# Block 1's attention with transposes ahead of scores, and copies ahead of row factors

## The reference, cut to what matters

```python
s_c = einsum(qb, k_c) * scale                      # 31 compressed blocks of keys
p_c = masked_softmax(s_c, c_end[None, :] <= tpos[:, None])
o_c = einsum(p_c, v_c)
...                                                # selected blocks: s_s, p_s, o_s
s_w = einsum(qb, kw) * scale                       # window of 512 keys
p_w = masked_softmax(s_w, m_w)
o_w = einsum(p_w, vw)
return gb[..., 0:1] * o_c + gb[..., 1:2] * o_s + gb[..., 2:3] * o_w
```

## Time and profile before

| | before |
|---|---|
| median of three runs | 2811.77 us |
| profiled execution, its own time | 2809.11 us |
| its span | 2807.3 us |
| TensorE busy (share of the span) | 2681.9 us (96%) |
| TensorE weight load | 2198.0 us (78%) |
| VectorE | 1571.4 us (56%) |
| ScalarE | 1055.5 us (38%) |
| GpSimd | 1178.2 us (42%) |
| attention of block 1 | 278 to 517 us of the span |

### The profile page before, as it was taken

How to read it: one execution, slowest core, us unless ns; L and a number is a source line. 1 busy time by engine, 2 the same in 40 slices (tenths; PEclk the granted TensorE clock), 3 DMA queues, 4 the chain that set the end, 5 groups by cost and what they waited for, 6 DMA issues and landing times.

```text
span 2807.3 us, 38071 instructions
## 1 busy us (share of the span) xinstructions
PE 2681.9 (96%) x13128; PEld 2198.0 (78%) x13128; DVE 1571.4 (56%) x2448; ACT 1055.5 (38%) x1826; POOL 1178.2 (42%) x592
## 2 busy tenths in 40 slices
PE   7999888899999999999999999999899999999998
PEld 6877666778888878878887788888687778888886
DVE  7996666564343376466665745545623447653364
ACT  4224777633222254443334411112525553211133
POOL 3432585244444444355423344444442214444443
PEclk9999999999999999999999999999999999999999
DMA  3242000133222232221102322222231112322222
GB/s 133 99 141 83 16 24 9 53 120 106 92 96 97 97 113 102 82 99 61 61 31 91 136 92 96 97 97 91 95 110 53 46 46 97 122 96 97 98 97 90
DMA packets 67460, 242.88 MB, mean 87 GB/s; under 512 B 7772, under 2 KB 10117, under 8 KB 66573
## 3 DMA queue, kind: packets, MB, share of 16 engines
q1 hardware_dynamic: 59760, 215.37, 22.6%
q10 hardware_dynamic: 7580, 25.91, 2.6%
HBM read 232.80 MB, written 6.35 MB: 85 GB/s over the span
## 4 chain that ended last, share of the span: by engine, by line
issue 47%; PE 34%; POOL 14%; DVE 2%; ACT 2%; POOLq 0%; DMA 0%; DVEq 0%; SPq 0%; ACTq 0%
POOL w_lo L442 12%; PE bank L2585 9%; PE bank L2587 9%; PE bank L2586 9%; PE bank L3133 2%; PE bank L3122 2%; POOL stat L469 1%; PE bank L2907 1%; POOL stat L466 1%; PE bank L2800 1%; PE bank L2894 0%; PE bank L2771 0%; ACT tmp L974 0%; DVE big L1925 0%; POOLq L446 0%
## 5 line engine op out<-in xcount | busy, mean ns | idle before, releaser
L442 POOL TENSOR_TENSOR w_lo<-raw,w_hi 128x1024 fp32r<-128x1024 f32 x398 | 972.4, 2443 | 1561.2 <-ACT w_hi L589 1439.9
L2585 PE MATMUL bank<-act,w_hi 128*128 128x512 f32 x3128 | 1259.0, 403 | 51.9 <-POOL w_lo L442 14.6
L2587 PE MATMUL bank<-act,w_lo 128*128 128x512 f32 x3128 | 1227.0, 392 | 0.0
L2586 PE MATMUL bank<-act,w_hi 128*128 128x512 f32 x3128 | 1226.6, 392 | 0.0
L589 ACT CAST w_hi<-raw 128x1024 fp32r<-128x1024 f32 x396 | 415.5, 1049 | 900.7 <-PE bank L2587 888.9
L2585 PEld LDWEIGHTS bank<-act,w_hi 128*128 128x128 f32 x3128 | 592.5, 189 | 199.7 <-issue 31.6
L2587 PEld LDWEIGHTS bank<-act,w_lo 128*128 128x128 f32 x3128 | 592.2, 189 | 126.9
L2586 PEld LDWEIGHTS bank<-act,w_hi 128*128 128x128 f32 x3128 | 592.9, 190 | 121.0 <-issue 5.5
L1685 DVE TENSOR_TENSOR X<-X,bank 128x512 f32 x56 | 38.5, 688 | 241.3 <-PE bank L2587 241.3
L2076 DVE CAST act<-tmp 128x512 f32 x64 | 142.4, 2225 | 10.0 <-DVE tmp L2072 5.2
L1837 DVE SCALAR_TENSOR_TENSOR bank<-big,cols,bank 128x512 f32<-128x512 f32 x174 | 117.0, 748 | 0.4
(11 more groups left out here) (427 smaller groups left out, 2962.5 us busy)
## 6 DMA issues: line engine op xcount, KB each, us to landing
raw<-in_w_dram SPq DMA_DIRECT2D x402, 512.0 KB, 3.4
act_f<-head_rows ACTq DMA_DIRECT2D x8, 768.0 KB, 4.2
proj_rows<-big ACTq DMA_DIRECT2D x4, 1024.0 KB
big<-proj_rows ACTq DMA_DIRECT2D x2, 2048.0 KB, 9.2
X<-in_x_dram SPq DMA_DIRECT2D x4, 512.0 KB, 6.1
act_f<-in_cw1k_dram ACTq DMA_DIRECT2D x4, 512.0 KB, 4.2
cst<-in_consts_dram ACTq DMA_DIRECT2D x2, 648.5 KB, 7.9
X<-big ACTq DMA_DIRECT2D x8, 128.0 KB, 3.4
```

Source lines behind the costliest of these rows:

```text
L442: pool.tensor_tensor(w_lo[:, u], raw[:, u].rearrange("p (k n) -> p k n", k=KT), w_hi[:, u].bitcast(F32), ALU.subtract).then_inc(w_lo_ready, 1)
L2585: pe.matmul(o, l_hi, r_hi, start=start, stop=False)
L2586: pe.matmul(o, l_hi, r_lo, start=False, stop=False)
L2587: return pe.matmul(o, l_lo, r_hi, start=False, stop=stop)
```

## The change

Three loops are written in another order. No instruction is added or taken away, and no wait changes.

```diff
@@ ScalarE
                     if n < N:
                         scale_rows(n)
+                    if n + 1 < N:
+                        exps(n + 1)
...
                     if n % 8 in (2, 4) and n // 8 + 1 < NH // 2:
                         compressed_exp(n // 8 * 2 + 2 + (n % 8 == 4))
-                    if n + 1 < N:
-                        exps(n + 1)
@@ VectorE
                 maxima(0)
+                maxima(1)
...
                 for n in range(N + 3):
+                    later = n // 8 + 1 < NH // 2
+                    if 2 <= n < N + 2:
+                        keep_second_pt(n - 2)
                     if n < N:
                         row_factor(n)
-                    if 2 <= n < N + 2:
-                        keep_second_pt(n - 2)
-                    if n + 1 < N:
-                        maxima(n + 1)
...
+                    if later and n % 8 in (1, 3):
+                        compressed_shift(n // 8 * 2 + 2 + (n % 8 == 3))
+                    if n + 2 < N:
+                        maxima(n + 2)
+                    if later and n % 8 in (4, 6):
+                        compressed_sum(n // 8 * 2 + 2 + (n % 8 == 6))
@@ TensorE
                 scores(0)
+                scores(1)
                 for n in range(N + 2):
                     if n < 6 * KT:
                         gate_filler(n)
-                    if n + 1 < N:
-                        scores(n + 1)
+                    if 1 <= n <= N:
+                        transposes(n - 1)
+                    if n + 2 < N:
+                        scores(n + 2)
                     if n % 8 in (0, 2) and n // 8 + 1 < NH // 2:
                         compressed_scores(n // 8 * 2 + 2 + (n % 8 == 2))
                     if n % 2 and n >= 3:
                         values(n - 3)
-                    if 1 <= n <= N:
-                        transposes(n - 1)
```

## The result

| | before | changed |
|---|---|---|
| median of the runs | 2811.14 us | 2846.15 us |
| profiled execution, its own time | 2809.11 us | 2844.81 us |
| its span | 2807.3 us | 2843.0 us |
| attention, causal mask of the first scores (0.3 us behind their start) to end | 277.6 to 517.0 us | 275.6 to 553.3 us |

A forecast was written before the change was run, and what follows sets the result against it. Waits going round between engines, none full, were taken to bound the attention. Octet terms of 4, 6.5, 4 and 2 us, together 16.5, on the profiled 2809.1 gave 2826 us (52%), range 2793 to 2842.

The forecast's parts named there:

- the clock: Attention: as many falls of the granted clock as before, costed at nothing, with bounds of 6 us either way.
- the wait of the maxima: Attention, step 4 of an octet: VectorE's maxima (1.2 us) and compressed sum (1.25) stand ahead of the copy TensorE needs.
- The views and the loop: Attention: waits going round between engines bound it; the loop for one pair sums to 6.95 us before, 6.84 after.
- The 36.7 us ahead of the values: TensorE's idle ahead of the values in the attention, expected to fall near nothing, with 50 to 60 us ahead of transposes.
- The sum for the order, 16.5 us: Attention: slower by 4 us in octet 0, 1.3 in each of octets 1 to 5, 4 in octet 6, 2 in octet 7.
- The copy of an even tile now starts at the end of the values: Attention: this copy must wait for the previous pair's values, leaving only the gate product to hide it before the next transposes.
- ScalarE's edit at nothing: Attention: exponentials moved earlier give back 0.3 to 0.6 us at three steps, not waited for, so costed at nothing.
- Octets 6 and 7 at 4 and 2 us: End of the attention: octet 6, without gate products, 4 us longer; octet 7, without cast and compressed work, 2 us longer.
- Faster: Rival: 36.7 us ahead of the values go, 19 come back ahead of transposes, 18 us less, 2791; chance 22%.
- No change: Rival: both loops hold the same work and an order adds no buffer, so 2809, within 5; chance 18%.
- Much slower: Rival: waits between VectorE's maxima and copies pass 2.5 us in every octet, the clock falling each time, 2840; chance 8%.
- The long factor: VectorE's two-element factor multiplication: 0.44 us on average, long while GpSimd's taps run, in both orders, difference the same.

The follow-up runs named there:

- e5: Changed kernel with VectorE's maxima one tile ahead instead of two, TensorE's scores still two ahead: 2804.05 us, 0.9985 of the kernel before.
- e7: Changed kernel with values ahead of transposes again and maxima one tile ahead: 2801.66 us, 0.9976 of the kernel before.
- e4: Changed kernel with only the values put back ahead of the transposes, maxima still two ahead: 2855.96 us, 1.0172 of the kernel before.
- e11: Changed kernel run once more, unaltered, for a second profile: 2861.51 us, 1.0176 of the kernel before.
- e9: Changed kernel plus three idle matmuls of 512 columns at each of the attention's last 18 steps: 2838.39 us, 1.0097 of the kernel before.
- e1: Kernel before with ScalarE's edit alone, exponentials ahead of the compressed one and the gate's copy: 2808.7 us, 0.9999 of the kernel before.
- e13: Kernel before with VectorE's copy ahead of the factor and ScalarE's edit: 2791.45 us, 0.9933 of the kernel before.
- e10: Kernel before plus three idle matmuls of 512 columns at each of the attention's last 18 steps: 2812.8 us, 1.0011 of the kernel before.
- e2: Kernel before with VectorE's copy ahead of the row factor alone, maxima and scores one ahead: 2793.08 us, 0.9947 of the kernel before.
- e6: Changed kernel with VectorE's factor ahead of the copy again, maxima still two ahead: 2862.81 us, 1.0187 of the kernel before.
- e12: Changed kernel with the factor's multiplication as two instructions of one tensor input each: 2838.23 us, 1.0102 of the kernel before.

## Why the prediction was wrong

Two steps failed: the clock, which was put at no change, and the wait of the maxima, which was counted in one step of eight and stands in nearly all.

**The views and the loop.** That the stage is bound by waits that go round was right. The 36.7 us ahead of the values went (0.8 left), and came back ahead of the transposes: 50.5, where 50 to 60 was predicted. Reciprocal, ScalarE's copies (38.7 us for values) and octets of 30 us or more came as written. Octet 6 "near 28" did not: 37.6.

**The sum for the order, 16.5 us.** The octets at full clock in both profiles give +1.0 (octet 3). Against the mean of before's octets at full clock with gate products, 29.15, the three at 31.9, 30.0 and 31.9 are 2.1 longer; predicted was 1.3. Taking 0.43 per us at half clock out, the attention is 277.7 - 24.7 = 253.0 against 239.4 - 5.5 = 233.9: about 19 us for the order (17 to 21 if half clock costs 0.48 or 0.38 instead). The size was nearly right, and the reason given for it mostly wrong. "The copy of an even tile now starts at the end of the values" is in the trace (L1941 waits 29.6 us for values), but with maxima one ahead the same place of the values costs nothing that can be told from none (e5, e7), and moving them back alone repairs nothing (e4: by the same reckoning its order costs some 36 us, with 40 at half clock). What costs is that maxima wait in front of the next copy for scores that TensorE issues behind the transposes. I had this wait at step 4 alone, where the compressed sum stands with it; it is there 57 times in 64.

**The step that put the number out of its range is the clock: "I expect as many falls as before", bounds 6 us either way.** Half clock went from 12.8 to 57.4 us, worth 0.43 x 44.6 = 19 us, and to 91.0 in the second profile, 34 us. The shares of order and clock add up, by the way they are taken, to the 38.3 us by which the attention is longer; it also starts 2.0 us earlier. The argument was "two idles of about 2 us in an octet" and so no change. The two are there: 16 idles of 1.8 us or more ahead of the transposes in eight octets, up to 4.0, and three ahead of scores. But the kernel before had only 8 so long in its whole attention, one in most octets, and e5 has 5. Their number alone doesn't decide: e11 has 19 as well, with 91.0 us at half clock instead of 57.4, and e4 has 18 with only 40. The runs don't show which property of the waits decides it. They show where: octets 6 and 7 in both profiles, with no gate product among the waits, and that matmuls put there bring the clock back (e9).

**ScalarE's edit at nothing** was right (e1, e13). **Octets 6 and 7 at 4 and 2 us** measured 11.2 and 15.2, most of it clock: in e9, with 3 x 0.24 us more in each step, they are at 31.3 and 38.2, 2.3 and 0.2 above e10.

**The rivals.** *Faster*, 2791, is what VectorE's copy first gives by itself, on TensorE's old order (2793, e2), but the same list moved the maxima, and that decided. *No change*: its rule from the Trainium skill (Perfetto Trace Analysis, Optimization Strategy), that a repeating gap can mean too few buffers, did not hold here. The runs disagree: with the same buffers, orders alone range from 2793 (e2) to 2863 (e6). *Much slower*, 2840 with 8%, had the right mechanism, waits around maxima and copies with the clock falling, and was nearest in time. It deserved more than 8%, since the walk through the steps had already found VectorE deciding at step 4.

**The long factor.** In the changed kernel it holds the handover now and then. A stretch on several engines:

```profile
357.00 2.35 POOL L442 TENSOR_TENSOR w_lo<-raw,w_hi 128x1024 fp32r<-128x1024 f32 x1 [4.83 <-ACT w_hi L589]
357.40 1.97 DVE L1932 TENSOR_TENSOR big<-big 128x2 f32<-128x2 f32 x1
359.40 0.91 ACT L983 ACTIVATE tmp<-tmp,big 128x256 f32<-128x256 f32 x2 [2.15 <-DVE big L1932]
360.03 0.47 PE L2857 MATMUL bank<-act,big_r 128*128 128x512 f32 x1 [2.00 <-DVE big L1955]
```

Two elements take 1.97 us, to the end of GpSimd's weight split. ScalarE's scaling waits 2.15 for them, and TensorE 2.00 for VectorE's next instruction. The prediction counted this as 0.44 on average in both orders. Its mean was 0.47 after, so the average hid single waits of 2 us, and three such stretches have scores that idle some 2 us behind them. This too is read from the trace, and e12 doesn't settle its price.

## What to carry to other kernels

Before hoisting an instruction on an in-order engine, ask when its input is issued and what then stands behind it: running two tiles ahead on the consumer is late, not early, if the producer issues that tile's input behind work that waits for the consumer. Split a change over several engines into its parts; here one part alone gave the gain (-15.6 us), and another, in the company of TensorE's new order, cost more than that. Where an edit makes TensorE's waits longer or more in a loop whose clock already falls now and then, price the clock as a term of its own, and let its upper bound be half clock in most of those octets that have least work on TensorE.

## What the runs showed of the hardware

- The same program ran at 2846.15 us in one set of runs and 2861.51 in another (the kernel before: 2811.14 and 2809.46), with 57.4 and 91.0 us at half clock in its attention. So this kernel's time is known to 0.5% only.
- More matmuls made a stretch shorter: 13 us of them added, 17.6 us gained in e9's last two octets, with the granted clock going from 0.82 and 0.69 to 0.95 and 1.00.
- A VectorE instruction with two SBUF tensors and two elements per partition took 160 ns at the least, 163 at the median and up to 2236 ns beside GpSimd (changed kernel). The 27 of its 64 instances that overlap no GpSimd instruction took 160 to 164; the three longest each end within 0.03 us of the weight split (L442) that runs beside them. With one tensor and one scalar operand it took 202 to 216 ns in 128 instances. The Trainium skill (GPSIMD Engine Reference, Specifications) names such contention with instructions that have two SBUF inputs; these rows agree.
